# Output gates of late tokens computed behind the first gather, in a one-core diffusion step

## What is computed

```python
q, f_fw, f_bw, v, g, xr, xg, ga, gb = jnp.split(h @ p['w_in'], IN_SPLITS, axis=-1)
o = _rmsnorm(o_fw + _flip(o_bw), p['hg_norm']) * jax.nn.silu(heads(g))
y_a = o.reshape(b, n, HG_VW).astype(h.dtype) @ p['w_branch_a']
y_b = (hr.astype(h.dtype) * jax.nn.gelu(xg)) @ p['w_branch_b']
merged = jax.nn.sigmoid(ga) * y_a + jax.nn.sigmoid(gb) * y_b
x = x + g1 * (merged @ p['w_out'])
...
# _peer: 8 heads x 16 experts a token, eidx from two top-16 lists
act = jax.nn.gelu(jnp.einsum('td,thkd->thk', hb, u_tab[eb]))
out = jnp.einsum('thk,thkd->td', gb * act, v_tab[eb])
```

## Time and profile before

| | us |
|---|---|
| median of 3 executions | 3947.18 |
| lowest, highest | 3942.33, 3949.27 |
| the profiled execution, its device time | 3947.58 |
| its span, first to last instruction | 3945.8 |
| busy: PE, DVE, POOL, ACT | 2948.1, 2783.8, 1305.9, 676.5 |
| POOL's wait ahead of its iota, just ahead of the gathers | 804.0 |
| mean granted clock of TensorE | 0.872 of 2.4 GHz |

### The profile page before, as it was taken

One profiled execution on the slowest core, in us unless ns is written; L12 is line 12 of the kernel. 1 busy time (PEld: TensorE's weight loads), 2 busy tenths in 40 slices (PEclk: granted clock), 3 DMA queues, 4 the chain that ended last, 5 costly groups with the idle time before them and its releaser, 6 DMA issues.

```text
span 3945.8 us, 46322 instructions
## 1 busy us (share of the span) xinstructions
PE 2948.1 (75%) x16906; PEld 1323.5 (34%) x16906; DVE 2783.8 (71%) x6805; ACT 676.5 (17%) x1391; POOL 1305.9 (33%) x1174
## 2 busy tenths in 40 slices
PE   8999999988799997856666666666656666665555
PEld 3665665545444442212322222212212222221111
DVE  4545546766787786747888768877877786887555
ACT  2534533011122120000111111110111111101000
POOL 0000000014443443433444434444444444444443
PEclk9999999989999998988888778778977788887777
DMA  4010003579999999999999999999999999999998
GB/s 184 24 35 26 24 25 149 184 255 409 416 414 411 415 402 418 417 422 411 404 399 414 414 408 411 417 404 419 415 412 411 410 415 408 414 415 411 420 417 338
DMA packets 214040, 1343.26 MB, mean 340 GB/s; under 512 B 24722, under 2 KB 45714, under 8 KB 62898
## 3 DMA queue, kind: packets, MB, share of 16 engines
q0 software_dynamic: 165888, 1208.03, 74.6%
q1 hardware_dynamic: 46628, 129.65, 8.8%
q10 hardware_dynamic: 1296, 2.62, 0.2%
HBM read 1326.55 MB, written 13.67 MB: 340 GB/s over the span
## 4 chain that ended last, share of the span: by engine, by line
DMA 37%; PE 36%; DVE 13%; issue 10%; POOL 3%; ACT 1%; POOLq 0%; SPq 0%; DVEq 0%; ACTq 0%
DMA arena<-in_uv,mask_b 13%; PE ps L794 12%; DMA arena<-in_uv,ones 11%; DMA arena<-in_uv,mask_f 11%; PE ps L1472 10%; DVE arena L1313 4%; PE ps L659 3%; PE ps L772 3%; POOL arena L628 3%; DVE arena L1193 2%; PE ps L1466 2%; PE ps L690 1%; PE ps L723 1%; DVE arena L1153 1%; PE ps L1524 1%
## 5 line engine op out<-in xcount | busy, mean ns | idle before, releaser
L794 PE MATMUL ps<-arena 64*64 64x512 f32 x9216 | 1458.8, 760 | 937.4 <-DVE arena L1193 925.5
L1313 DVE CUSTOM_DVE_ANT_0 arena<-arena 128x1024 f32<-128x1024 f32 x1152 | 1410.9, 1225 | 737.0 <-DMA arena<-in_uv,mask_b 286.8
L794 PEld LDWEIGHTS ps<-arena 64*64 64x64 f32 x9216 | 351.2, 158 | 1885.7 <-DVE arena L1193 1374.1
L628 POOL DMA_INDIRECT arena<-in_uv,ones x384 | 440.7, 1148 | 621.5 <-PE ps L794 480.5
L628 POOL DMA_INDIRECT arena<-in_uv,mask_f x384 | 435.3, 1134 | 591.3 <-PE ps L794 502.9
L628 POOL DMA_INDIRECT arena<-in_uv,mask_b x384 | 424.1, 1104 | 593.9 <-PE ps L794 505.7
L988 ACT ACTIVATE arena<-arena 128x2 f32<-128x2 f32 x576 | 117.1, 203 | 2639.8 <-DVE arena L1313 2570.2
L1472 PE MATMUL ps<-arena 128*128 128x384 f32 x1152 | 384.3, 490 | 1.8 <-DVE arena L1759 1.8
L1193 DVE TENSOR_SCALAR arena<-arena 128x64 f32<-128x64 f32 x1152 | 307.4, 309 | 0.4 <-ACT arena L988 0.3
L772 PE MATMUL ps<-arena 128*128 128x384 f32 x768 | 269.0, 497 | 0.0
L610 POOL IOTA arena<- 128x16 f32 x1 | 0.1, 144 | 804.0 <-PE ps L672 804.0
(11 more groups left out here) (209 smaller groups left out, 2367.7 us busy)
## 6 DMA issues: line engine op xcount, KB each, us to landing
arena<-in_w_mg SPq DMA_DIRECT2D x16, 1536.0 KB, 17.0
arena<-in_w_in SPq DMA_DIRECT2D x28, 512.0 KB, 3.3
arena<-in_w_mod SPq DMA_DIRECT2D x8, 1792.0 KB
arena<-in_w_mod SPq DMA_DIRECT2D x4, 2048.0 KB, 23.4
arena<-in_w_out SPq DMA_DIRECT2D x2, 4096.0 KB, 17.1
arena<-in_w_q SPq DMA_DIRECT2D x8, 1024.0 KB, 15.5
arena<-in_w_q SPq DMA_DIRECT2D x4, 2048.0 KB, 36.2
arena<-in_uv,ones POOLq DMA_INDIRECT x384
```

The source lines that it names most:

```text
L628: nc.gpsimd.indirect_dma_start(out=RG[n % RING], out_offset=None, in_=uv, in_offset=bass.IndirectOffsetOnAxis(ap=EIDX[t % 3][:, s:s + 1], ...
L794: mm = nc.tensor.matmul(PS[c * HALF:(c + 1) * HALF, 2 * r + n, :], DG[rows, s, :], RG[s][rows, D + n * 512:D + (n + 1) * 512], start=(g == ...
L1313: ins = v.tensor_tensor_reduce(u, u, h2, 1.0, 0.0, ALU.mult, ALU.add, PRE[:, s % RING:s % RING + 1])
```

## The change

The late 768 tokens of the output gates of heads 0 to 2 (two thirds of `B_G` and two of `B_XG` each) are no longer projected in the scan. There `oA` and `hB` hold the ungated values at first, and 12 units (3 heads, 2 gates, 2 thirds) are projected in stage B. `put_off` does it: 8 matmuls a unit on TensorE, banks 5 and 7 in turn, silu or gelu on ScalarE into one buffer, a product in place on VectorE. They run five matmuls a group in groups 21, 24, 27 and 30, and in groups 31 to 46. Their weights, 6 blocks of 512 KB, are loaded again by SP into buffers of the query weights, head 0's after query 7, head 1's after query 10, both ahead of scores (1,0), head 2's after query 12 and behind scores (1,0). The first third of each gate stays in the scan.

In the scans of heads 0 to 2 the filler is now 5 thirds: one of `B_G`, one of `B_XG`, and the three of the next head's `B_FF`. Steps 16 and 17 have none. Heads 1 to 3 then start with `B_Q`, and `turn_head` comes after its second third. Head 3 keeps six thirds. The number of each third, by which the waits count, comes from a table (`Z_NUMBER`, `z_done`). The late merge moves 12 groups back, to groups 47 to 123, the output projection to 129, and the start of tile 3's norm and queries from group 152 to 164, of tile 4's from 192 to 204. `EARLY_TOP_AT` is the same. SP's order is otherwise the same. The core of the diff:

```diff
@@ -106,17 +106,38 @@
 QUERY_AT = lambda n: 1 + 3 * (n - 2)
-MERGE_AT, MERGE_STEP = 35, 5
-MIX_AT, MIX_STEP = 117, 3
+PUT_AT, PUT_STEP, PUT_REST = (21, 24, 27, 30), 5, 31
+MERGE_AT, MERGE_STEP = 47, 5
+MIX_AT, MIX_STEP = 129, 3
 EARLY_TOP_AT = {(0, 0): None, (0, 1): 0, (0, 2): 18, (0, 3): 27, (1, 0): 37, (1, 1): 47, (1, 2): 65, (1, 3): 78,
                 (2, 0): 90, (2, 1): 100, (2, 2): 110, (2, 3): 129}
-LATE_AT = {3: 2 * GROUPS + 24}
+LATE_AT = {3: 2 * GROUPS + 36, 4: 3 * GROUPS + 12}
 LATE_GAP = {3: 10}
-def late_chunk(c):
-
-    return (B_G, B_XG)[c // NCH], c % NCH
+def scan_units(h):
+
+    if h < PUT_OFF:
+        return [(h, B_G, 0), (h, B_XG, 0)] + [(h + 1, B_FF, n) for n in range(NCH)]
+    return [(h, b, n) for b in (B_G, B_XG) for n in range(NCH)]
+
+
+def z_numbers():
+
+    order = [(0, B_FF, n) for n in range(NCH)]
+    for h in range(HEADS):
+        order += [(h, b, n) for b in range(B_Q, B_G) for n in range(NCH)]
+        order += scan_units(h)
+    return {u: c for c, u in enumerate(order)}
+
+
+Z_NUMBER = z_numbers()
+Z_ALL = len(Z_NUMBER)
+
+
+def z_done(h, b):
+
+    return 1 + max(c for (hh, bb, n), c in Z_NUMBER.items() if (hh, bb) == (h, b))
 def wait_alone(eng, sem, value):
@@ -301,6 +322,9 @@
     PIECE_IN = (2, 3, 0, 1, 4, 2, 3, 0)
+    PUT_IN = [MG[:, :, TA + n * PIECE:TA + (n + 1) * PIECE] for n in (1, 2, 0)]
+    PUT_W = lambda d, kind, k: PUT_IN[d][:, kind * 4 + k // 2, (k % 2) * P:(k % 2 + 1) * P]
+    PUT_TMP = AR[:, A_SIG:A_SIG + CH]
     KEYS_IN = strips[:, 8:16, 0:PIECE]
@@ -406,6 +433,17 @@
         return MERGE_AT + n // MERGE_STEP
+    def put_group(n):
+        early = PUT_STEP * len(PUT_AT)
+        return PUT_AT[n // PUT_STEP] if n < early else PUT_REST + (n - early) // PUT_STEP
+
+    def put_unit(u):
+
+        d, r = divmod(u, 4)
+        return d, r // 2, 1 + r % 2
+
+    PUT_UNITS = 4 * PUT_OFF
+
     def mix_group(n):
@@ -516,9 +554,18 @@
         piece(6)
+        def put_off(d, queries):
+            sp.wait_ge(q_r, queries)
+            for kind, b in enumerate((B_G, B_XG)):
+                sp.dma_start(PUT_IN[d][:, kind * 4:kind * 4 + 4],
+                             w_in[d, W_BLOCKS.index(b)].rearrange("p (r k) c -> p r (k c)", k=2)).then_inc(l_put[d], 16)
+
         sp.wait_ge(q_r, 7)
         piece(7)
+        put_off(0, 7)
+        put_off(1, 10)
         score_in(1, 0)
+        put_off(2, len(QUERY_ORDER))
         sp.wait_ge(q_r, len(QUERY_ORDER))
@@ -754,6 +801,22 @@
             mm.then_inc(sc_r, 1)
+        def put_off(n):
+
+            u, k = divmod(n, KD)
+            d, kind, part = put_unit(u)
+            bank = (5, 7)[u % 2]
+            if k == 0:
+                pe.wait_ge(l_put[d], l_put0 + 32)
+                if u >= 2:
+                    pe.wait_ge(put_e, put_e0 + u - 1)
+                elif u == 1:
+                    pe.wait_ge(h2t_e, EARLY)
+            mm = nc.tensor.matmul(PS[:, bank, 0:CH], PUT_W(d, kind, k), hT[:, k, part * CH:(part + 1) * CH],
+                                  start=(k == 0), stop=(k == KD - 1))
+            if k == KD - 1:
+                mm.then_inc(put_r, 1)
+
         def merge_late(n):
@@ -907,8 +974,17 @@
             A(BEST, BEST, ACT.Exp).then_inc(ge_r, 1)
+        def put_off(u):
+            kind = put_unit(u)[1]
+            act.wait_ge(put_r, u + 1)
+            if u:
+                act.wait_ge(put_m, put_m0 + u)
+            A(PUT_TMP, PS[:, (5, 7)[u % 2], 0:CH], (ACT.Silu, ACT.Gelu_apprx_tanh)[kind]).then_inc(put_e, 1)
+
         def merge_late(c):
             act.wait_ge(mg_gates, c + 1)
+            if c == 0:
+                act.wait_ge(put_m, put_m0 + PUT_UNITS)
             if c < 2:
@@ -1036,6 +1114,12 @@
             v.tensor_tensor(MROW2[u], PS[0:2, 4 * u + 3, :], BROW2[u], ALU.add).then_inc(m_evac, 1)
+        def put_off(u):
+            d, kind, part = put_unit(u)
+            dve.wait_ge(put_e, put_e0 + u + 1)
+            to = (oA, hB)[kind][:, d, part * CH:(part + 1) * CH]
+            v.tensor_tensor(to, to, PUT_TMP, ALU.mult).then_inc(put_m, 1)
+
         def merge_late(c):
@@ -1446,17 +1532,20 @@
             def z_bank(b, n):
-                c = h * ZC + b * NCH + n
+                return bank_of(h, b, n)
+
+            def bank_of(hz, b, n):
+                c = Z_NUMBER[hz, b, n]
                 if c >= 2:
                     pe.wait_ge(z_free, c - 1)
-                return z_of(h, b, n)
-
-            def project(b, n, ks=range(KD)):
+                return z_of(hz, b, n)
+
+            def project(hz, b, n, ks=range(KD)):
                 if ks[0] == 0:
-                    pe.wait_ge(l_w[W_BLOCKS.index(b)], h * 16 + 16)
-                    z_bank(b, n)
-                z = z_of(h, b, n)
+                    pe.wait_ge(l_w[W_BLOCKS.index(b)], hz * 16 + 16)
+                    bank_of(hz, b, n)
+                z = z_of(hz, b, n)
                 w = W[:, W_BLOCKS.index(b)]
@@ -1467,17 +1556,17 @@
                     for k in ks:
-                        if h == 0 and b == B_FF and n == 0:
+                        if hz == 0 and b == B_FF and n == 0:
                             pe.wait_ge(h_ready, k + 1)
                     mm.then_inc(z_ready, 1)
-            for b in (B_FF, B_Q, B_FB, B_XR, B_V):
+            for b in (B_FF, B_Q, B_FB, B_XR, B_V)[min(h, 1):]:
                 for n in range(NCH):
-                    project(b, n)
-                    if h and b == B_FF and n == 1:
+                    project(h, b, n)
+                    if h and b == B_Q and n == 1:
                         turn_head(h - 1)
@@ -1500,7 +1589,8 @@
                     c, part = divmod(it - GATE_STEPS, 2)
-                    project(*late_chunk(c), range(part * KD // 2, (part + 1) * KD // 2))
+                    if c < len(scan_units(h)):
+                        project(*scan_units(h)[c], range(part * KD // 2, (part + 1) * KD // 2))
             def scores(it):
@@ -1653,15 +1744,19 @@
                         ins.then_inc(z_free, 1)
-                elif (it - GATE_STEPS) % 2:
-                    b, n = late_chunk((it - GATE_STEPS) // 2)
-                    out, func = ((oA, ACT.Silu), (hB, ACT.Gelu_apprx_tanh))[b == B_XG]
-                    evac(b, n, out[:, h, n * CH:(n + 1) * CH], func).then_inc(z_free, 1)
+                elif (it - GATE_STEPS) % 2 and (it - GATE_STEPS) // 2 < len(scan_units(h)):
+                    hz, b, n = scan_units(h)[(it - GATE_STEPS) // 2]
+                    sl = slice(n * CH, (n + 1) * CH)
+                    if b == B_FF:
+                        evac(b, n, SG[0][:, sl], ACT.Sigmoid, hz=hz).then_inc(z_free, 1)
+                    else:
+                        out, func = ((oA, ACT.Silu), (hB, ACT.Gelu_apprx_tanh))[b == B_XG]
+                        evac(b, n, out[:, h, sl], func).then_inc(z_free, 1)
             def decay(it):
                 if it == GATE_STEPS:
-                    act.wait_ge(z_free, h * ZC + B_G * NCH)
+                    act.wait_ge(z_free, z_done(h, B_G - 1))
                     for d in range(2):
@@ -1893,18 +1988,26 @@
                 v.tensor_tensor(o, o, scale.unsqueeze(2).to_broadcast([P, CH // P, P]), ALU.mult).then_inc(on_r, 1)
-            dve.wait_ge(z_free, (h + 1) * ZC)
+            dve.wait_ge(z_free, z_done(h, B_XG))
             hc = hB[:, h, 0:N_CTX]
             hl = hB[:, h, N_CTX:T].rearrange("p (r c) -> p r c", c=GRID_W)
-            v.tensor_tensor(hl, hl, I[0][:, N_CTX:T].rearrange("p (c r) -> p r c", r=GRID_H),
-                            ALU.mult).then_inc(lru_done, 1)
+            il = I[0][:, N_CTX:T].rearrange("p (c r) -> p r c", r=GRID_H)
+            gated = (TA - N_CTX) // GRID_W if h < PUT_OFF else GRID_H
+            ins = v.tensor_tensor(hl[:, 0:gated], hl[:, 0:gated], il[:, 0:gated], ALU.mult)
+            if h < PUT_OFF:
+                ins = v.tensor_copy(hl[:, gated:], il[:, gated:])
+            ins.then_inc(lru_done, 1)
             for n in range(NCH):
                 oc = oA[:, h, n * CH:(n + 1) * CH]
-                v.scalar_tensor_tensor(out=oc, in0=turned(n), scalar=pr[:, h, P_HN:P_HN + 1], in1=oc,
-                                       op0=ALU.mult, op1=ALU.mult).then_inc(hg_done, 1)
+                if n and h < PUT_OFF:
+                    ins = v.tensor_scalar(oc, turned(n), pr[:, h, P_HN:P_HN + 1], None, ALU.mult)
+                else:
+                    ins = v.scalar_tensor_tensor(out=oc, in0=turned(n), scalar=pr[:, h, P_HN:P_HN + 1], in1=oc,
+                                                 op0=ALU.mult, op1=ALU.mult)
+                ins.then_inc(hg_done, 1)
         stage_b_dve(dve)
```

More of the change, by code:

```diff
@@ L68 @@
 NB = len(W_BLOCKS)
-ZC = B_END * NCH
+PUT_OFF = HEADS - 1
 TI = 2 * TILES
@@ L210, in build @@
     tanh_w = sem("tanh_written")
-    t_ready, w1_ready = sem("modT_ready"), sem("w1_ready")
+    t_ready = sem("modT_ready")
     sq_a = sem("squares_added")
@@ L245, in z_of @@
     def z_of(h, b, n):
-        return PS[:, (h * ZC + b * NCH + n) % 2, 0:CH]
```

(23 more changed lines are left out.)

12 lines of the change are left out of this document (6 added, 6 removed).

## The result

The changed kernel is slower. Its median is 3961.45 us (3949.95 to 3967.11, 15 runs) against 3944.47 us (3939.33 to 3951.64, 15 runs) for the kernel before: a ratio of 1.0043, 95% interval 1.0035 to 1.0051, or 17 us more where I had forecast 29 us less (3918 us). The profiled execution took 3959.81 us, its span is 3958.0.

What follows compares the result with a forecast made beforehand. TensorE was taken to bound the kernel before the gathers, full DMA engines from about 880 us; -46.4 - 3.9 + 8 + 2 + 10 + 4 - 3 = -29.3 us gave 3918 us, range 3899 to 3937.

Steps and rivals of the forecast that it cites:

- part 1: Between two scans: the first block of heads 1 to 3 leaves a stretch where TensorE is full, saving 46.4 us.
- part 2: In the scan, last two steps without filler: the last output follows VectorE's last update sooner, saving 3.9 us.
- Rival C: Merge groups after a wait: TensorE stays at 1.2 GHz, 10.6 us a group for 5.3; 8 groups give 3960; chance 0.04.
- part 3: DMA bytes: six weight blocks of 512 KB loaded a second time, 3.15 MB, cost 8 us.
- part 4: TensorE behind the gather: put-off matmuls fit; an 8 us wait for their weights, covered by gathers, costs 2 us.
- part 5: SP's queue after the 12-group shift: late score loads cost 10 us at (1,3), 4 us for four other selections together.
- part 6: Start of tile 4: its norm moves off the end of tile 2, where VectorE is full, saving 3 us.
- B: Merge groups: TensorE as full as DMA, so score-load waits are never made up; +16 us on the forecast, 3934; chance 0.16.
- A: Late score loads: cost nothing as DMA carries merge weights meanwhile; the lost 14 us vanish, 3904; chance 0.25.
- D: Between scans: VectorE, not TensorE, sets the pace, so half of part 1 is lost, 3941; chance 0.05.

## Why the prediction was wrong

- **Between two scans** (part 1): right. Nothing but projections stands in the chain there, and with TensorE kept warm the two parts gave the 50 us that I forecast (iota at 754.5).
- **In the scan** (part 2): the size was right, a condition was missing. The last output did start when I said, at 203.4 us. I hadn't asked at which clock it and the next head would run after 3.26 us of waiting: the first projections take 11.7 to 12.9 us for 10.5. 42 us came instead of 50. Rival C's mechanism was real, but I had put it in the merge groups, where the clock is low for one group after a wait (0.50 in 1295 to 1300, 1.00 from 1305 on). That its 3960 us are so near the 3961 measured is chance: no run of groups at the low level stands in the trace.
- **Bytes** (part 3): not measured by itself. The terms that were, -42.9 + 10.4 + 36.2 + 4.4, leave 9 us to the 17 measured, near the 8 that I took. But four differences of medians stand in that, and it is good to some 12 us only.
- **TensorE behind the gather** (part 4): the matmuls fit, nearly as forecast (383 to 387 GB/s from 960 to 980 us with the wait gone, with TensorE busy throughout). The wait was 10.6 us for a forecast 8. The step that failed is "with six gathers in flight to cover it: 2 us". It cost 10.4, above my bound of 8.
- **Late score loads** (part 5): the step from SP's order to the waits was right. The term was mis-sized: 14 us, measured 36. For (1,3) I had 10 us of empty engines, and the trace has about that; it cost 15.6 by the medians and 14 by the rows, since the engines also ran below their pace afterwards. For the four others the step that failed is "waits of 7 to 15 us with 15 us of gathers in flight, 0 to 4 each": I let them hide all but 4 us, and some 20 were lost.
- **Tile 4's start** (part 6): the gain at the end of tile 2 is there (338 for 303 GB/s over 20 us, 1.7 us), but the selections of tile 4 then ran over the end of tile 3, which I hadn't followed: 4 us lost. The sign was wrong.
- **The rivals.** B named the nearer result for the score loads, with a reason that is only part of it: long waits in a stretch where TensorE is idle a third of the time cost no less of their length. Its sum doesn't follow from its words either. Three waits in full would be 37 to 53 us by my own sizes, 23 to 39 on top of the 14, and it says 16; measured, the score loads cost 22 us more than in my sum and the put-off weights 8. A fell: a wait of 5 us over which the gathers ran on the earlier trace rows says nothing of one of 20. D fell: in the changed kernel TensorE's projections (line 1561) waited 1.8 us in all, and with the filling spread evenly the heads came down to 132 us.

Forecast and measurement are 46 us apart. The scans are 8 of them, the put-off weights 8, the score loads 22 and the tile boundaries 6; the rest is within what the medians can tell.

One error is under part 4 and the four shorter waits of part 5: I set the wait alone against the gathers in flight. What decides how long the DMA engines are empty is the wait and the way back to the next gather, less what is in flight. In my sum for (1,3) the way back stands, with 8 us; in the other two sums I left it out. In the run with three long waits, 19.6 us of wait and 6.5 us of way back, less 9 us, give the 17 us in which the engines were nearly empty. And what was in flight at the wait's start were those 9 us, not the 15 of six gathers. So flight and way back nearly cancel, and about the length of the wait is left. How much less than its length a wait costs is not well known: 9 us in 45, 4 to 5 in 20 and 5 in 61 by the medians, each good to 5 us or more.

## What to carry to other kernels

In a ring that keeps the bounding engine full, price a wait of any stage at nearly its length: the engine runs on at its start for little longer than it stands empty behind its end. Do so whether or not the waiting engine has reserve. When work is moved to other groups, go through every queue that carries its loads in a fixed order, and put those loads first whose reader stands ahead of the bound. Empty steps in a loop of small matmuls cost clock behind them: spread what is left evenly.

## What the runs showed of the hardware

A small load lands late while a large one is on its way on SP. In the run with all score loads first, here are loads of 256 KB of scores and merge weights of 1.5 MB in SP's timeline, and the landings of the score loads issued at 1216.8, 1352.0 and 1407.6 us:

```profile
1215.47 0.54 SPq L551 DMA_DIRECT2D arena<-in_w_mg  x1
...
1216.81 1.81 SPq L546 DMA_DIRECT2D arena<-score_scratch  x1
...
1322.44 0.56 SPq L551 DMA_DIRECT2D arena<-in_w_mg  x1
1352.00 0.33 SPq L546 DMA_DIRECT2D arena<-score_scratch  x1
...
1407.58 0.33 SPq L546 DMA_DIRECT2D arena<-score_scratch  x1
```

```profile
DMA to landing us min/median/max: 32.2/32.2/32.2
...
DMA to landing us min/median/max: 8.6/8.6/8.6
...
DMA to landing us min/median/max: 7.3/7.3/7.3
```

All three are the same kind of load beside full gathers. The first is issued 1.3 us behind a block of weights that takes 26.7 us to land, and lands after 32.2 us. The others are issued when the block ahead of them (28.1 and 27.3 us to landing) has just landed, and land after 8.6 and 7.3. The run's eight score loads part in this way: four with a block of merge weights on its way, 26.0 to 35.0 us; four without, 7.3 to 8.6. In the changed kernel those of (2,0), (2,1) and (2,2) are issued within a microsecond of a block, and land after 29.2, 28.7 and 30.2 us. So SP's order made the loads late twice: it held up their issue, and it put 1.5 MB ahead of them. Only the order was changed in a run, not the size of what stands ahead, so the cause is read from the traces. A transfer of 256 KB from memory to memory, with nothing large on its way, landed after 5.5 us.
